# Two fused transformer blocks: gate tiles moved among the stick-breaking items, an own buffer for the first gates, and a new schedule of late rows

## The chip, the cores and the metric

The kernel runs on one core of one Trainium2 chip. TensorE (PE) does the matrix products, VectorE (DVE), ScalarE (ACT) and GpSimd (POOL) the rest, and SyncE (SP) issues most transfers. The metric is the time of one execution in microseconds on the device: 2365.03 us is the median of three runs before the change (2364.62 to 2365.92).

## The reference, cut to what matters

Two blocks work on 512 tokens of width 1024. The first ends in a layer of 16,384 experts: each token scores two lists of 128 keys per head, picks 16 experts for each of 8 heads, and mixes them. The second has two attentions side by side, each followed by a gate.

```python
def peer_ffn(h, wq, sub_keys, u, v):          # 8 heads, top 16 of 128 x 128 experts
    q = (t @ wq).reshape(PEER_BLOCK, PEER_HEADS, 2, PEER_DQ // 2)
    s = jnp.einsum('tpcd,pckd->tpck', q, sub_keys)
    s1, i1 = lax.top_k(s[:, :, 0], PEER_TOPK);  s2, i2 = lax.top_k(s[:, :, 1], PEER_TOPK)
    top, pos = lax.top_k(cand, PEER_TOPK)     # cand = all sums s1 + s2
    g = jax.nn.softmax(top, axis=-1)
    a = jax.nn.gelu(jnp.einsum('tpkd,td->tpk', u[idx], t), approximate=False)
    return jnp.einsum('tpk,tpkd->td', g * a, v[idx])

# second block
o_a = stick_breaking_attention(...)           # w = sigmoid(z) * prod of sigmoid(-z) to the right
y_a = (o_a * jax.nn.silu(sb_z)) @ w_branch_a
o_b = latent_attention(...)                   # softmax; y_b in the same manner
x = x + gate * ((sigmoid(g_a) * y_a + sigmoid(g_b) * y_b) @ w_out)
```

## The kernel before, in words

All products are done in a split form: each float32 operand is cut into a high and a low part, and `split3` (L1081) issues three matmuls, high by high, high by low and low by high. ACT writes the high part (`high`), DVE or POOL the rest (`low`).

**The experts.** 384 of the 512 tokens go through all experts, in groups of two tiles of 128 experts (48 matmuls of 384 columns). `phase_peer` counts groups g from 0 to 75: 4 for an output projection, 8 for the queries, and then 64 for the first half, in which PE multiplies tokens by `u` and ACT takes gelu. The result does not fit into the on-chip memory, so `spill` writes it to DRAM. The second half is `down(g)`, 64 groups again: the gelu is read back, multiplied by the gates (`weigh`, L1713), split and multiplied by `v`. The gates come from DVE's selection (`select`, 16 units up to group 36), from one-hot products (`batch` on DVE, `spread` on PE, 48 batches from group 41 to 68), and from DRAM, where they are kept between (`gate_pair`, L1248, one transfer for two groups).

The last 128 tokens don't take that way. POOL fetches for each of 128 picks the row of `u` or `v` that each token wants (`rows_by_index`, into a ring of five buffers), and DVE takes a dot product with it (`dot`) or adds it up (`row`). Each engine runs one program in order. What decides the place of a pick is `pick_step` (POOL's request), `dot_step` (DVE's dot, a group later) and `row_step` (the rows of `v`), and `batch_place` does so for the gates. Up to group 40 POOL also makes the low part of `u` (L1305), from group 41 on DVE does (L1685).

**The second block.** After the projections the attention goes through 32 pairs of items, one pair in each of `slots` = 34 slots: 16 pairs of stick-breaking items, then 16 of softmax items, with queries against 128, 256, 384 and 512 keys in turn. In slot p PE computes the scores of pair p, then the tiles that `fill[p]` holds, then the values of pair p-2 and the transposes of pair p-1. DVE masks both items, does its part of the fill tiles (`low`, `evac`) and then finishes both items (for stick: a scan L2349 and a product L2352). ACT takes the sigmoids or exponentials (L2188, L2189, L2191), then `high` and its part of the fill. `second_tiles` lists the tiles and their weight pieces in order. A tile `uqm` has 3 products of 128 rows, `kn` and `kv` have 2, `ga` and `sz` 8, `bra` 4; each product is three matmuls of 512 columns. `early` and `late` spread the tiles over the slots by their number.

## Time and profile before

| | us |
|---|---|
| median of three runs | 2365.03 |
| the profiled execution | 2369.11 |
| its span, first to last instruction | 2367.3 |
| PE busy in the span | 2206.1 |
| DVE busy | 1684.8 |
| ACT busy | 918.6 |
| POOL busy | 617.9 |

The first half of the experts ends near 1297 us on the profile's clock, the second near 1827. The attention slots lie between 1967 and 2215. A wait is put down to what came last.

### The profile page before, as it was taken

Reading aid. Unit: us, or ns where it says so; the run is one execution under the profiler, and the core shown is the slowest. Engines: PE = TensorE matmul, PEld = TensorE weight load, DVE = VectorE, ACT = ScalarE, POOL = GpSimd, SP = SyncE. Lnnn points to the kernel's source line nnn. Section 1 sums busy time; section 2 is a strip of 40 time slices with the busy share of each in tenths; the row PEclk is TensorE's granted clock in tenths of the full one; section 3 lists DMA queues with packets and bytes.
Section 4 is the critical chain, followed back from the end, with each engine's and each line's share of the span. In section 5 each row is a group of like instructions: output and inputs, shape, how many; then the busy total and the mean of one; then the engine's idle time right before and its main releaser. Section 6 shows DMA issues by size and latency. Waiting matters only on the chain. (4 is left out here: it accounts for less than half of the span.)

```text
span 2367.3 us, 31784 instructions
## 1 busy us (share of the span) xinstructions
PE 2206.1 (93%) x12629; PEld 1966.4 (83%) x12629; DVE 1684.8 (71%) x2801; ACT 918.6 (39%) x1203; POOL 617.9 (26%) x354
## 2 busy tenths in 40 slices
PE   5999889988999998999999899999999896899997
PEld 2888777866799998999999899999999674576775
DVE  6555677873489999889876778788786656756543
ACT  4222234333233333566653233333333533576323
POOL 0000042322347667233333433333331000000000
PEclk8999999999999999999999999999999898899999
DMA  7567410012237777899999999999995222111222
GB/s 257 206 227 236 154 50 1 1 71 72 89 125 250 242 243 244 300 370 334 364 339 382 361 352 353 351 359 349 350 362 209 82 89 71 54 54 63 80 89 72
DMA packets 178100, 488.69 MB, mean 206 GB/s; under 512 B 13696, under 2 KB 80384, under 8 KB 166432
## 3 DMA queue, kind: packets, MB, share of 16 engines
q1 hardware_dynamic: 141088, 352.43, 43.6%
q0 software_dynamic: 36864, 134.23, 14.7%
q8 instruction: 100, 1.64, 0.3%
q14 instruction: 48, 0.39, 0.1%
HBM read 432.08 MB, written 52.43 MB: 205 GB/s over the span
## 5 line engine op out<-in xcount | busy, mean ns | idle before, releaser
L1087 PE MATMUL ps<-h_high,u_high 128*128 128x384 f32 (+1 forms) x1216 | 429.7, 353 | 21.7 <-POOL u_low L1305 11.9
L1089 PE MATMUL ps<-h_high,u_low 128*128 128x384 f32 (+1 forms) x1216 | 421.3, 346 | 0.0
L1088 PE MATMUL ps<-h_low,u_high 128*128 128x384 f32 (+1 forms) x1216 | 421.2, 346 | 0.0
L1087 PE MATMUL ps<-w_high,v_high 128*128 128x384 f32 x1024 | 343.6, 336 | 10.4 <-DVE w_low L1722 10.4
L1089 PE MATMUL ps<-w_high,v_low 128*128 128x384 f32 x1024 | 342.8, 335 | 0.0
L1088 PE MATMUL ps<-w_low,v_high 128*128 128x384 f32 x1024 | 342.8, 335 | 0.0
L1087 PEld LDWEIGHTS ps<-h_high,u_high 128*128 128x128 f32 x1216 | 231.5, 190 | 35.9 <-POOL u_low L1305 13.8
L1455 ACT ACTIVATE v_high<-v_raw 128x2048 fp32r<-128x2048 f32 x64 | 122.6, 1916 | 346.6 <-PE ps L1089 346.6
L1087 PE MATMUL ps<-h_high,w_high 128*128 128x512 f32 x560 | 226.7, 405 | 22.3 <-DVE w_low L346 7.5
L1089 PEld LDWEIGHTS ps<-h_high,u_low 128*128 128x128 f32 x1216 | 231.1, 190 | 8.1
L1088 PEld LDWEIGHTS ps<-h_low,u_high 128*128 128x128 f32 x1216 | 232.0, 191 | 7.1
L1088 PE MATMUL ps<-h_low,w_high 128*128 128x512 f32 x560 | 220.4, 394 | 0.0
L1089 PE MATMUL ps<-h_high,w_low 128*128 128x512 f32 x560 | 220.3, 393 | 0.0
L1710 DVE TENSOR_TENSOR v_low<-v_raw,v_high 128x2048 fp32r<-128x2048 f32 x64 | 146.7, 2292 | 101.6 <-ACT v_high L1455 101.6
L1293 POOL DMA_INDIRECT mixT<-in_peer_v,row_index x102 | 145.4, 1425 | 252.1 <-DVE row_sum L1754 236.0
L1293 POOL DMA_INDIRECT mixT<-in_peer_u,row_index x103 | 143.2, 1391 | 236.2 <-DVE row_dot L1680 214.3
L1087 PEld LDWEIGHTS ps<-w_high,v_high 128*128 128x128 f32 x1024 | 192.9, 188 | 10.9 <-DVE v_low L1710 9.8
L1088 PEld LDWEIGHTS ps<-w_low,v_high 128*128 128x128 f32 x1024 | 192.9, 188 | 0.0
L1089 PEld LDWEIGHTS ps<-w_high,v_low 128*128 128x128 f32 x1024 | 192.8, 188 | 0.0
L1531 ACT ACTIVATE gelu<-ps 128x384 f32<-128x384 f32 x128 | 62.9, 492 | 322.1 <-PE ps L1089 199.2
L2267 DVE TENSOR_TENSOR w_low<-w_raw,w_high 128x1024 fp32r<-128x1024 f32 x69 | 84.6, 1226 | 133.8 <-ACT w_high L2139 133.6
L1087 PEld LDWEIGHTS ps<-h_high,w_high 128*128 128x128 f32 x560 | 106.4, 190 | 55.1 <-DVE w_low L2267 10.2
(434 smaller groups left out, 4192.5 us busy)
## 6 DMA issues: line engine op xcount, KB each, us to landing
v_raw<-in_peer_v SPq DMA_DIRECT2D x64, 1024.0 KB
w_raw<-in_w SPq DMA_DIRECT2D x99, 512.0 KB, 3.5
u_first<-in_uT SPq DMA_DIRECT2D x32, 1024.0 KB
u_second<-in_uT SPq DMA_DIRECT2D x32, 1024.0 KB
xT<-in_late_w SPq DMA_DIRECT2D x56, 512.0 KB, 4.4
gelu_up<-gelu SPq DMA_DIRECT2D x128, 192.0 KB
gates<-gates_sb SPq DMA_DIRECT2D x12, 2048.0 KB, 12.6
weighted<-gelu_up SPq DMA_DIRECT2D x64, 384.0 KB
```

The source lines that it names most:

```text
L1087: pe.matmul(out, wh, mh, start=start, stop=False)
L1088: pe.matmul(out, wh, ml, start=False, stop=False)
L1089: return pe.matmul(out, wl, mh, start=False, stop=stop)
L1293: pool.indirect_dma_start(out=row_of(total), out_offset=None, in_=table, in_offset=bass.IndirectOffsetOnAxis(ap=row_no[:, n:n + 1], axis=0))\
L1455: act.activation(v_high[:, g % 2], v_raw[:, g % 2], ACT.Copy).then_inc(v_hi, 1)
L1531: act.activation(gel[:, x % 4, :], ps[:, x % 4, 0:DENSE], ACT.Gelu).then_inc(u_ev, 1)
L1710: dve.tensor_tensor(v_low[:, g % 2], v_raw[:, g % 2], v_high[:, g % 2].bitcast(F32), ALU.subtract)\
L2267: dve.tensor_tensor(wlo[:, i % SPLITS, :], raw[:, i % RAWS, :], whi[:, i % SPLITS, :].bitcast(F32), ALU.subtract).then_inc(w_low, 1)
```

## The change: what it does, and the diff

- Picks: 34 picks (40 before) go to the groups 16 to 40, 76 (66) to the groups 41 to 68, and 18 (22) to the end, which now starts at group 68. The last dots fall in group 75, not after it. POOL issues the picks of a group after the low part of the next group, not before it.
- The first batch of gates is one tile later, and the rows of `v` start in the second group of the second half.
- gelu is spilled three groups after it, not four.
- The even gate pairs have a buffer of their own, `first_gates`, so the first can be loaded without waiting for a buffer of `u`. The odd ones use `u_first`.
- ACT and DVE prepare groups 0 and 1 of the second half ahead of the sums over picked rows.
- In the second block the order of the tiles is new: three of the four `sz` and two of the eight `ga` now stand among the stick items; tiles are spread by their products, not their number; `uq` has two heads in a piece, so there are four pieces fewer.
- The score of each item waits for its own bank alone, and DVE masks the item n+2 right behind finishing item n.

```diff
-EARLY, MIDDLE = 40, 66
+EARLY, MIDDLE = 34, 76
-    return GROUPS - 7 + 7 * (n - EARLY - MIDDLE) // (PICKS - EARLY - MIDDLE)
+    return GROUPS - 8 + 7 * (n - EARLY - MIDDLE) // (PICKS - EARLY - MIDDLE)
-    return SPREAD_AT * EXPERT_TILES + m * SPREAD_G * EXPERT_TILES // BATCHES
+    return SPREAD_AT * EXPERT_TILES + 1 + m * (SPREAD_G * EXPERT_TILES - 1) // BATCHES
-    return n * (U_G - 3) // PICKS
+    return 1 + n * (U_G - 4) // PICKS
...
+        first_gates = sb("gates_in", [P, BLOCKS * 2 * GE * TB])
-        gr = [x[:, 0:BLOCKS * 2 * GE * TB].rearrange("p (n j t) -> p n j t", n=BLOCKS, j=2 * GE) for x in u_raw]
+        gr = [x[:, 0:BLOCKS * 2 * GE * TB].rearrange("p (n j t) -> p n j t", n=BLOCKS, j=2 * GE)
+              for x in (first_gates, u_raw[0])]
...
-                if g - 4 >= OUT_G + WQ_G:
-                    spill(g - 4)
+                if g - 3 >= OUT_G + WQ_G:
+                    spill(g - 3)
...
-            spill(GROUPS - 4)
+            gate_pair(0)
             load(0)
-            sp.wait_ge(u_split, OUT_PIECES + WQ_G + U_G - 1)
-            gate_pair(0)
             spill(GROUPS - 3)
             load(1)
             spill(GROUPS - 2)
-            sp.wait_ge(u_split, OUT_PIECES + WQ_G + U_G)
+            sp.wait_ge(u_split, OUT_PIECES + WQ_G + U_G - 1)
             gate_pair(1)
...
-            for x in range(WQ_G + U_G):
+            for x in range(WQ_G + U_G + 1):
...
-                for n in picks_at[x + OUT_G]:
+                for n in picks_at[x + OUT_G - 1]:
...
+            high_v(1)
+            high_w(1)
             act.wait_ge(row_used, PICKS)
             act.activation(row_dot[:], row_dot[:], ACT.Gelu).then_inc(row_gelu, 1)
...
-    for i in range(2):
-        piece("kn", i, [("kn", 4 * i + j) for j in range(4)])
+    piece("kn", 0, [("kn", j) for j in range(4)])
+    piece("ga", 0, [("ga", 0)])
+    piece("sz", 0, [("sz", 0)])
+    piece("kn", 1, [("kn", 4 + j) for j in range(4)])
+    piece("ga", 1, [("ga", 1)])
     piece("kv", 0, [("kv", t) for t in range(4)])
-    for i in range(8):
+    for i in (1, 2):
+        piece("sz", i, [("sz", i)])
+    halfway = len(tiles)
+    for i in (2, 3):
         piece("ga", i, [("ga", i)])
...
+        for first, end, slot, count in ((PROJECTED, HALFWAY, 0, HALF), (HALFWAY, ATTENDED, HALF, slots - HALF)):
+            sizes = [PRODUCTS2[TILES2[j][0]] for j in range(first, end)]
+            for x, j in enumerate(range(first, end)):
+                fill[slot + sum(sizes[:x]) * count // sum(sizes)].append(j)
...
-                if p:
-                    pe.wait_ge(acted, 2 * p)
                 for s in range(2):
+                    if p:
+                        pe.wait_ge(acted, 2 * p - 1 + s)
...
-                dve.wait_ge(scored, 2 * (n // 2) + 2)
+                dve.wait_ge(scored, n + 1)
...
-                if p < PAIRS:
-                    finish(2 * p)
-                    finish(2 * p + 1)
+                for n in (2 * p, 2 * p + 1):
+                    if n < N:
+                        finish(n)
+                    if n + 2 < N:
+                        mask(n + 2)
```

DVE at the end of the experts' first half, before: from the last dot but one to the split of the second group of the second half (`weighted` is the gelu times the gates).

```order
L1680 ISA row_dot 128x1
L1680 ISA mixT,row_dot<-mixT,h_by_token 128x1024
L1680 ISA row_dot 128x1
L1760 TENSOR_TENSOR row_weight<-row_dot,row_gate 128x128
L1757 TENSOR_SCALAR row_sum<-mixT,row_weight 128x1024
L1754 SCALAR_TENSOR_TENSOR row_sum<-h_by_token,row_weight,row_sum 128x1024
L1754 SCALAR_TENSOR_TENSOR row_sum<-mixT,row_weight,row_sum 128x1024
L1718 TENSOR_TENSOR weighted<-weighted,u_first 128x768
L1710 TENSOR_TENSOR v_low<-v_raw,v_high 128x2048
L1722 TENSOR_TENSOR w_low<-weighted,w_high 128x768
```

The same place in the changed kernel:

```order
L1680 ISA row_dot 128x1
L1718 TENSOR_TENSOR weighted<-weighted,gates_in 128x768
L1710 TENSOR_TENSOR v_low<-v_raw,v_high 128x2048
L1722 TENSOR_TENSOR w_low<-weighted,w_high 128x768
L1718 TENSOR_TENSOR weighted<-weighted,gates_in 128x768
L1710 TENSOR_TENSOR v_low<-v_raw,v_high 128x2048
L1722 TENSOR_TENSOR w_low<-weighted,w_high 128x768
L1761 TENSOR_TENSOR row_weight<-row_dot,row_gate 128x128
L1758 TENSOR_SCALAR row_sum<-mixT,row_weight 128x1024
L1755 SCALAR_TENSOR_TENSOR row_sum<-h_by_token,row_weight,row_sum 128x1024
```

The split of the second group moved ahead of the first three rows of `v`, and no dot stands between the splits.

DVE among the stick items, before: one slot with a weight piece, from its masks to the masks of the next.

```order
L2335 TENSOR_TENSOR ps<-ps,causal_mask 128x128 x2
L2267 TENSOR_TENSOR w_low<-w_raw,w_high 128x1024
L2349 SCALAR_TENSOR_TENSOR at_prod<-at_rest,zeros 128x383
L2352 TENSOR_TENSOR at_w<-at_w,at_prod 128x384
L2349 SCALAR_TENSOR_TENSOR at_prod<-at_rest,zeros 128x383
L2352 TENSOR_TENSOR at_w<-at_w,at_prod 128x384
L2335 TENSOR_TENSOR ps<-ps,causal_mask 128x128 x2
```

And in the changed kernel slot 7, with the tile `sz` 0 (`gate_tmp`, `stick_out`, `g_low`):

```order
L2279 TENSOR_TENSOR w_low<-w_raw,w_high 128x1024
L2301 TENSOR_TENSOR gate_tmp<-ps,gate_tmp 128x512
L2303 TENSOR_TENSOR stick_out<-stick_out,gate_tmp 128x512
L2305 TENSOR_TENSOR g_low<-stick_out,g_high 128x512
L2361 SCALAR_TENSOR_TENSOR at_prod<-at_rest,zeros 128x511
L2364 TENSOR_TENSOR at_w<-at_w,at_prod 128x512
L2347 TENSOR_TENSOR ps<-ps,causal_mask 128x128
L2361 SCALAR_TENSOR_TENSOR at_prod<-at_rest,zeros 128x511
L2364 TENSOR_TENSOR at_w<-at_w,at_prod 128x512
L2347 TENSOR_TENSOR ps<-ps,causal_mask 128x128
```

The masks of the next pair stand between and behind the two finishes, and three operations of a gate tile came in.

## Rows read from the trace of the kernel before

**Rows 1.** Waits of PE over the whole execution: who waited for whom, us, times, longest.

```profile
PE ps L1087 <- DVE w_low L2267: 16.4, 13, 5.3
PE ps L1087 <- POOL u_low L1305: 11.9, 9, 2.8
PE ps L1087 <- DVE w_low L1722: 10.4, 2, 9.5
```

**Rows 2.** Busy time by stretch, stick and softmax slots: PE, PEld, DVE, ACT, POOL, PEclk, DMA.

```profile
1967.00:2086.00 119.00, 88.33 (x448) 56.56 (x447) 83.38 (x141) 60.92 (x139) 0.00 (x0) 0.86 0.17 52
2086.00:2218.00 132.00, 127.68 (x708) 97.23 (x707) 77.58 (x195) 81.40 (x145) 0.00 (x0) 1.00 0.20 65
```

**Rows 3.** Timeline of DVE among the stick items: start, us, instruction, idle before and releaser.

```profile
1970.70 0.50 DVE L2335 TENSOR_TENSOR ps<-ps,causal_mask 128x128 f32<-128x128 f32 x2 [5.15 <-PE ps L2072]
...
1999.47 0.50 DVE L2335 TENSOR_TENSOR ps<-ps,causal_mask 128x128 f32<-128x128 f32 x2
2002.84 1.23 DVE L2267 TENSOR_TENSOR w_low<-w_raw,w_high 128x1024 fp32r<-128x1024 f32 x1 [2.87 <-ACT w_high L2139]
...
2006.24 1.22 DVE L2349 TENSOR_TENSOR_SCAN at_prod<-at_rest,zeros 128x511 f32<-128x511 f32 x1
...
2010.28 0.50 DVE L2335 TENSOR_TENSOR ps<-ps,causal_mask 128x128 f32<-128x128 f32 x2
...
2081.02 0.29 DVE L2337 TENSOR_TENSOR ps<-ps,causal_mask 128x128 f32<-128x128 f32 x1
```

**Rows 4.** Waits of DVE from 1966 to 2090 us: us, times, longest.

```profile
DVE w_low L2267 <- ACT w_high L2139: 22.5, 11, 2.9
...
DVE at_prod L2349 <- ACT at_rest L2189: 4.7, 6, 1.0
```

**Rows 5.** Timeline of PE: fill products, the first softmax scores, the last values.

```profile
2041.17 0.39 PE L1088 MATMUL ps<-g_low,w_high 128*128 128x512 f32 x1
2041.40 0.39 PE L1089 MATMUL ps<-g_high,w_low 128*128 128x512 f32 x1
...
2078.64 0.68 PE L2072 MATMUL ps<-mqkv 96*128 96x128 f32 x4 [1.21 <-ACT at_rest L2189]
...
2213.94 1.09 PE L2091 MATMUL ps<-at_wT,mqkv 128*64 128x128 f32 x16
```

**Rows 6.** Timeline of POOL in the selection stage.

```profile
774.18 1.70 POOL L1293 DMA_INDIRECT mixT<-in_peer_u,row_index  x1 [5.20 <-DVE row_dot L1680]
```

**Rows 7.** Timeline around group 40, of DVE, POOL and PE.

```profile
924.37 0.56 DVE L1659 TENSOR_TENSOR peer_sel<-peer_top 128x384 f32<-128x384 f32 x1
...
930.34 4.76 POOL L1305 TENSOR_TENSOR u_low<-u_first,u_high 128x2048 fp32r<-128x2048 f32 x1
...
943.90 1.23 DVE L1680 CUSTOM_DVE_ANT_0 row_sum<-row_sum,h_by_token 128x1024 f32<-128x1024 f32 x1 [3.89 <-DMA row_sum<-in_peer_u,row_index]
...
948.67 1.86 PE L1348 MATMUL ps<-gated_one_hots,one_hots 128*128 128x128 f16 x16 [3.57 <-DVE gated_one_hots L1704]
```

**Rows 8.** Groups of DVE instructions from 700 to 960 us: count, busy us, mean ns, idle before.

```profile
L1644 DVE TENSOR_TENSOR peer_half<-peer_pos,peer_cuts 128x32 uint32<-128x32 uint32 x12 | 20.7, 1728 | 0.4
```

**Rows 9.** Timeline of PE, one of four such waits in groups 41 to 68.

```profile
1011.58 1.08 PE L1348 MATMUL ps<-gated_one_hots,one_hots 128*128 128x128 f16 x16 [0.28 <-issue]
```

**Rows 10.** Timeline of PE, group 72 and the second group of the second half.

```profile
1262.03 0.60 PE L1087 MATMUL ps<-h_high,u_high 128*128 128x384 f32 x1 [2.52 <-DVE u_low L1685]
...
1316.56 0.52 PE L1088 MATMUL ps<-w_low,v_high 128*128 128x384 f32 x1
1316.88 0.52 PE L1089 MATMUL ps<-w_high,v_low 128*128 128x384 f32 x1
```

**Rows 11.** Busy time by stretch, as in rows 2, in the second half of the experts.

```profile
1350.00:1400.00 50.00, 50.00 (x290) 50.00 (x289) 40.42 (x32) 15.90 (x12) 18.49 (x14) 1.00 0.99 356
```

**Rows 12.** Timeline of DVE, a row of `v` ahead of the second group's split.

```profile
1310.74 1.28 DVE L1754 SCALAR_TENSOR_TENSOR row_sum<-mixT,row_weight,row_sum 128x1024 f32<-128x1024 f32 x1 [3.35 <-DMA mixT<-in_peer_v,row_index]
```

**Rows 13.** Timeline of SP: the load of `v` for the third group.

```profile
1304.19 0.38 SPq L1254 DMA_DIRECT2D v_raw<-in_peer_v  x1
```

More of the change, by code:

```diff
@@ L1228, in spill @@
                     sp.dma_start(gelu[g - OUT_G - WQ_G][:, j, :], gel[:, x % 4, :]).then_inc(spilled[x % 4], 16)
-            written = 0
-            for g in range(GROUPS):
-                if g >= 2:
-                    sp.wait_ge(u_split, PIECES_BEFORE + g - 1)
-                if g:
-                    sp.dma_start(u_raw[g % 2][:], raw_of(g)).then_inc(u_in[g % 2], 16)
-                if g == 3:
-                    sp.dma_start(keys[:], k.dram["keysT"]).then_inc(keys_in, 16)
-                if g - 4 >= OUT_G + WQ_G:
-                    spill(g - 4)
-                while written < BLOCKS and g >= batch_place(PER_BLOCK * (written + 1) - 1) // GE + 4:
-                    sp.wait_ge(evac, 2 * PER_BLOCK * (written + 1))
-                    sp.dma_start(k.gates[:, written], gs[:, written % 2]).then_inc(wrote[written % 2], 16)
-                    written += 1
-            assert written == BLOCKS
-            for r in range(2):
-                sp.wait_ge(wrote[r], 16 * (BLOCKS // 2))
             def gate_pair(i):
@@ L1257, in load @@
                 sp.dma_start(w[:, g % 2], gelu[g]).then_inc(w_in[g % 2], 16)
-            spill(GROUPS - 4)
+            written = 0
+            for g in range(GROUPS):
+                if g >= 2:
+                    sp.wait_ge(u_split, PIECES_BEFORE + g - 1)
+                if g:
+                    sp.dma_start(u_raw[g % 2][:], raw_of(g)).then_inc(u_in[g % 2], 16)
+                if g == 3:
+                    sp.dma_start(keys[:], k.dram["keysT"]).then_inc(keys_in, 16)
+                if g - 3 >= OUT_G + WQ_G:
+                    spill(g - 3)
+                while written < BLOCKS and g >= batch_place(PER_BLOCK * (written + 1) - 1) // GE + 4:
+                    sp.wait_ge(evac, 2 * PER_BLOCK * (written + 1))
+                    sp.dma_start(k.gates[:, written], gs[:, written % 2]).then_inc(wrote[written % 2], 16)
+                    written += 1
+            assert written == BLOCKS
+            for r in range(2):
+                sp.wait_ge(wrote[r], 16 * (BLOCKS // 2))
+            gate_pair(0)
             load(0)
-            sp.wait_ge(u_split, OUT_PIECES + WQ_G + U_G - 1)
-            gate_pair(0)
             spill(GROUPS - 3)
@@ L1533, in _ @@
                     high(g + 2 - OUT_G)
+            high_v(1)
+            high_w(1)
             act.wait_ge(row_used, PICKS)
             act.activation(row_dot[:], row_dot[:], ACT.Gelu).then_inc(row_gelu, 1)
-            for g in range(1, U_G):
+            for g in range(2, U_G):
                 high_v(g)
@@ L1742, in _ @@
                         batch(m)
-            weigh(0)
-            low_v(0)
-            low_w(0)
+            for g in range(2):
+                weigh(g)
+                low_v(g)
+                low_w(g)
             for n in dots_at[GROUPS]:
@@ L1964, in width, with first_gate @@
             return (items[n][2] + 1) * P
-        early, late = list(range(PROJECTED, tile_no("ga", 0))), list(range(tile_no("ga", 0), ATTENDED))
         slots = PAIRS + 2
+        soft_ready = tile_no("kv", 3) + 1
         fill = {p: [] for p in range(slots)}
-        for x, j in enumerate(early):
-            fill[x * HALF // len(early)].append(j)
-        for x, j in enumerate(late):
-            fill[HALF + x * (slots - HALF) // len(late)].append(j)
+        for first, end, slot, count in ((PROJECTED, HALFWAY, 0, HALF), (HALFWAY, ATTENDED, HALF, slots - HALF)):
+            sizes = [PRODUCTS2[TILES2[j][0]] for j in range(first, end)]
+            for x, j in enumerate(range(first, end)):
+                fill[slot + sum(sizes[:x]) * count // sum(sizes)].append(j)
+        def first_gate(n):
+            return mo[:, 2 + n, :] if n < EARLY_GA else merged[:, n, :]
         @block.sync
@@ L2036, in tile @@
                         pe.wait_ge(t_low, G0 + 5)
-                    w3, src = weights(j, 0, 3), [(ghi[:, t, :], glo[:, t, :]) for t in range(3)]
+                    w3, src = weights(j, 3 * (n % 2), 3), [(ghi[:, t, :], glo[:, t, :]) for t in range(3)]
                 elif kind == "kn":
@@ L2419, in _ @@
             dve.wait_ge(made, 3)
+            mask(0)
+            mask(1)
             for p in range(slots):
-                if p < PAIRS:
-                    mask(2 * p)
-                    mask(2 * p + 1)
                 for j in fill[p]:
```

29 lines of the change are left out of this document (15 added, 14 removed).

## The prediction

> **What bounds the kernel now.** I read PE's waits first. The longest sums are three: weight splits in the second block (16.4 us), POOL's low parts in the experts' first half (11.9 us), and the split of the first two groups of the second half (10.4 us, one of them 9.5) [rows 1]. Then the busy time by stretch: in the second half of the experts PE is never idle [rows 11], so nothing is to be had there; in the softmax slots it is busy 127.7 us of 132, but in the stick slots 88.3 of 119 [rows 2]. So PE is the bound in the softmax slots and something else is in the stick slots. The timeline of DVE tells what: DVE masks both items, waits 2.87 us for ACT (sigmoids of both items, then the high part of a weight piece), splits it and finishes both items, and the next masks stand right behind [rows 3]. The 16 stick slots are this loop, 1970.7 to 2081.0, 110.3 us.
>
> All sums are against the profiled execution (2369.1 us, its span 2367.3). The median is 4.1 us below that, and I take the same difference off at the end.
>
> **Selection stage, groups 16 to 41.** POOL waits for DVE's dots before it may ask for rows (5.20 us in the row shown [rows 6]) and does PE's low part behind that. The change takes POOL's order apart and leaves DVE fewer dots, so PE's 11.9 us [rows 1] should go. But they come back: at group 38 ACT waits for DVE's last selection, and DVE is full up to there (subtraction of the maxima at 924.37, then the exponential, ACT's high part, and POOL's low part for group 40 from 930.34 to 935.10 [rows 7]). PE arrives sooner and waits there in one piece. What counts is how much sooner DVE ends: dots up to group 36 are 28 in place of 32, 4 x 1.15 us = 4.6 us (each row dot starts 1.15 us after the one before; 1.23 us is the instruction [rows 7]). Behind it stands the wait of 3.57 us for the first gate batch [rows 7]. With the batch one tile later it would be gone, but the pick of group 39 is now asked for only after the low part of group 40. Its dot then stands ahead of the low part of group 41, and such a row took some 8 us from its request (DVE waited 3.89 us of them [rows 7]). By hand, from the time at which group 40 may start: wait for the row 8.3, dot 1.15, low 2.2, dot 1.15, gate parts 0.95, batch 2.45, low 2.2, three dots 3.45, batch 2.45 = 24.3 us to the second batch. PE gets to group 42 some 4 us sooner than before, less 1.5 us for a slow clock after its long wait. I take -3; bounds -9 (the 3.57 and 4.6 both won, and the slow clock not met) to +4 (row and clock both cost once more).
>
> The slow clock is seen in rows: behind the wait of 2.52 us, as behind the one of 9.5 us, about 10 to 12 matmuls start 0.32 us apart, twice the 0.172 us of the steady stretch (290 in 50 us) [rows 10, 11]. Each such wait costs 1.5 to 1.8 us more. Waits up to 1.9 us show none.
>
> **Groups 42 to 68.** 76 dots in place of 66. Before, 10 groups had three dots, now 20 of 28. A group of PE is 48 x 0.172 = 8.3 us and 1.08 per batch [rows 9, 11], so 10.4 with two batches and 9.4 with one. DVE starts its low part 2.5 us after PE starts the group before (ACT's high part lies between); with three dots and a batch it is done at 2.5 + 2.2 + 3.45 + 2.4 = 10.55. Behind a group with two batches PE waits 0.1 to 0.28 us, which is what the four short waits before show [rows 9]; behind a group with one batch, 1.15. The new pattern has four such places (groups 46, 50, 54, 58): 4.6 us, and a little of the short ones. I take +5, bounds 0 and +9 (all 20 groups at 0.45).
>
> **Late rows.** The wait of 2.52 us at group 72 comes from a dot whose row was 13 us under way, behind a burst of four requests and a gate write. Now the burst stands at group 69 and the rows of group 71 are asked for earlier. 2.5 + 1.5 for the clock = -4; bounds -4 and 0.
>
> **Into the second half.** Before: 0.9 and 9.5 us of waits [rows 1] and 1.8 for the clock, 12.2 us. The 9.5 goes, since DVE no longer waits for rows of `v` (3.35 and 3.4 us [rows 12]) ahead of the second split. What is late next is the third group: its `v` is loaded only after all gelu is stored (1304.19 before, some 6 us after the second half began [rows 13]), and PE wants it 16.6 us after the beginning, less the high part 1.9, low part 2.3 and the product's low part 0.95: it has 5 to 6 us to land. 1.4 MB (1 MB of `v`, 0.4 of gelu) at about 200 GB/s beside the row requests is 7 us. I count 0.5 + 0.5 + 2.7 us of waits for groups 0, 1, 2, 1 us of clock and 0.5 later, 5.2 us. Net -7; bounds -12 (nothing is late) and -1. The sooner gates and sooner spill I cost at nothing: the transfers stand in one queue and the DMA engines are busy 0.99 of the time [rows 11], so a sooner issue mostly waits in the queue.
>
> **Stick slots.** The fill of the stick slots grows from 48 to 88 products, at 3 x 0.23 us [rows 5] 27.6 us of PE, into 30.7 us of PE idle time. But DVE is the bound there. Busy on DVE: one more piece (12 for 11, 1.2 us) and three `sz` tiles at 3 x 0.69 us, +7.5 us. Idle on DVE: ahead of a low part it now waits for the sigmoids of one item, not two: about 2.15 for 2.87 us at 512 keys, but there are 11 such waits in place of 9, and one behind two `kn` tiles: +1.2 on the 20 to 22 us [rows 4]. The three `sz` wait for their tile (5.5 us of PE), its sigmoid and the copy between their products: +5.6. The waits for the sigmoids ahead of a finish go: -4.7 [rows 4]. In three slots (12 or 8 products beside little DVE work) PE is last: +4. Together +14, so PE reaches the softmax scores at about 2092, not 2078.6 [rows 5]. Bounds: 0 (the new order of masks hides all) and +27.6 (nothing hidden).
>
> **Softmax slots.** PE took 2078.64 to 2215.0, 136.4 us [rows 5], of which 128 products are 88.3 us. Now 88 products: 60.7, with the same rest of 48.1 is 108.8; four slots have no fill, where the chain of mask, exponential and finish shows, about 0.5 us each: 110.8. -26; bounds -27.6 and, if that chain sets the pace of every slot, 0. Six table loads fewer on ACT (1.28 us each) lie beside PE and give nothing. The attention together: -12.
>
> **Sum.** -3 + 5 - 4 - 7 - 12 = -21: 2348.1 for a profiled execution, 2344 for the median.
>
> **Rivals.**
> 1. *The gates are hidden wholly.* For: 30.7 us of idle PE in the stick slots, and masks that no longer wait for both items. Against: DVE is busy 83 of 119 us there, and its idle time is ACT's chain, which stays. Attention -25 in place of -12: 2331.
> 2. *The experts give nothing.* The waits taken away come back as later ones: DVE at +9 in groups 42 to 68, the third group late by 6 us. For: DMA share 0.99 and DVE busy up to 45 of 50 us. Then -1 from the experts and -12: about 2354 with middle values, up to 2360.
> 3. *DVE is held up by POOL (slower).* The tiny operation L1644, 32 columns, takes 1.73 us on average, more than a scan over 511 columns (1.22) [rows 3, 8]: it waits for something that ends, and 12 of them are 20.7 us. Today POOL is in step with DVE. When POOL's order is taken apart it falls elsewhere. If each of 11 selections lost 2.3 us more, the last would end 25 us later, PE would wait at group 40, and the time would be 2344 + 25 = 2369. It decides from a mean of about 3.5 us for that operation. The Trainium skill (SBUF — State Buffer, section "Who interferes with whom") says that a DVE instruction with two inputs in SBUF and a GpSimd instruction that reads SBUF exclude each other for the whole instruction; by that rule the phase between the two engines sets this price. The long mean agrees with it. It could as well get better.
> 4. *The softmax slots keep their pace (slower).* If mask, table load, exponential and finish take as long per slot as the 8 products did, the 136.4 us stay and the stick slots cost 14: 2344 + 26 = 2370. Against: DVE is busy 77.6 and ACT 81.4 of 132 us there.
>
> **How the numbers follow.** The forecast (2336 to 2354) has 0.52, rival 1 0.15, rival 2 0.16, rivals 3 and 4 together 0.09, and 0.08 goes to sums that end within 0.2% of 2365 (4.7 us, about what a measurement can tell). The range 2328 to 2363 takes in part of rival 1 and nearly all of rival 2. Faster: 0.52 + 0.15 + 0.16 = 0.83; same 0.08; slower 0.09.
>
> **What would show it.** No wait above 1 us on POOL's low parts before group 38, and one of 5 us or more at group 40. Short waits of about 1 us at groups 46, 50, 54 and 58. No wait of 2.5 us near group 72. The second group of the second half starts within 1 us of the end of the first, the third is 1 to 5 us late. First softmax scores 14 us later than the same place before, counted from the first mask, with DVE's low parts still waiting for ACT; then some 111 us to the last values. The forecast is wrong if the stick slots take under 115 or over 135 us, if the softmax slots stay above 120 us, or if L1644 goes above 3 us.

## The result: 0.5% slower, and the profile after

The changed kernel took 2380.91 us (median of 11 runs, 2374.2 to 2385.8), the kernel before 2369.19 us in the same session (2364.4 to 2372.6). The ratio is 1.0047, 95% interval 1.0038 to 1.0057: about 11 us slower. I had forecast 2344 us and gave "slower" 0.09.

Stretches of the two profiled executions, cut at the same work of PE in both:

| from ... to | before | after | difference | forecast |
|---|---|---|---|---|
| start to the fourth score product (L1336, then L1334) | 670.7 | 668.0 | -2.7 | 0 |
| to the transposes of group 40 | 264.9 | 290.5 | +25.6 | -3 (bounds -9 to +4) |
| to the first product of the second half | 362.5 | 367.0 | +4.5 | +1 |
| to the end of the second half | 549.8 | 541.8 | -8.0 | -7 |
| to the first stick scores | 122.2 | 122.0 | -0.2 | 0 |
| stick slots, to the first softmax scores | 108.6 | 128.9 | +20.3 | +14 |
| softmax slots, to the last values | 136.4 | 108.4 | -28.0 | -26 |
| to the end of the span | 152.3 | 152.6 | +0.3 | 0 |

So all of the loss, and more, lies in one stage of the experts, the one in which DVE selects rows. First the waits of PE over the whole execution, which answer to [rows 1]:

```profile
PE ps L1087 <- POOL u_low L1303: 20.0, 6, 8.1
PE ps L1395 <- DVE peer_sel L1739: 17.9, 1, 17.9
...
PE ps L1346 <- issue: 6.9, 7, 2.2
...
PE ps L1087 <- DVE soft_out L2291: 6.9, 3, 3.2
...
PE ps L1087 <- DVE w_low L2279: 2.6, 4, 1.5
...
PE ps L1087 <- DVE w_low L1722: 1.8, 1, 1.8
```

The 9.5 us into the second half are gone (1.8 left), and so are most of the 16.4 us for low parts of weights in the second block. But the waits for POOL's low parts have grown from 11.9 to 20.0 us, and there is a new one of 17.9 us. They stand here (timeline of PE in the changed kernel):

```profile
827.82 0.69 PE L1087 MATMUL ps<-h_high,u_high 128*128 128x384 f32 x1 [8.04 <-POOL u_low L1303]
...
912.97 0.69 PE L1087 MATMUL ps<-h_high,u_high 128*128 128x384 f32 x1 [8.05 <-POOL u_low L1303]
...
958.48 2.18 PE L1395 MATMUL ps<-ident,peer_sel 128*128 128x128 f32 x9 [17.93 <-DVE peer_sel L1739]
```

PE waits for POOL, POOL (8.74 us at 821.38) for DVE's row dots, and DVE waits for nothing in this stage: from 690 us to its end no gap on DVE is above 0.15 us. So the question is why DVE's operations take longer. Groups of DVE instructions from 700 to 960 us, as in [rows 8]; columns are count, busy us, mean ns, idle before. Of the changed kernel:

```profile
L1680 DVE CUSTOM_DVE_ANT_0 mixT<-mixT,h_by_token 128x1024 f32<-128x1024 f32 x26 | 43.0, 1691 | 0.3
L1622 DVE TENSOR_TENSOR peer_indf<-peer_ind,peer_cuts 128x64 f16<-128x64 uint32 x11 | 23.6, 2145 | 0.4
L1644 DVE TENSOR_TENSOR peer_half<-peer_pos,peer_cuts 128x32 uint32<-128x32 uint32 x12 | 17.6, 1463 | 0.4
```

And of the kernel before, beside its L1644 in [rows 8]:

```profile
L1622 DVE TENSOR_TENSOR peer_indf<-peer_ind,peer_cuts 128x64 f16<-128x64 uint32 x11 | 5.3, 478 | 0.4
```

L1622 writes 64 columns and takes 0.23 us when nothing is in its way. Now it takes 2.1 us on average. One case shows what it collides with. DVE, then POOL, in the changed kernel:

```profile
828.52 5.04 DVE L1622 TENSOR_TENSOR peer_indf<-peer_ind,peer_cuts 128x64 f16<-128x64 uint32 x1
833.48 0.68 DVE L1627 TENSOR_TENSOR peer_cand<-peer_val 128x512 f32<-128x512 f32 x1
```
```profile
823.07 4.69 POOL L1303 TENSOR_TENSOR u_low<-u_second,u_high 128x2048 fp32r<-128x2048 f32 x1
827.91 0.96 POOL L1291 DMA_INDIRECT mixT<-in_peer_u,row_index  x1
828.89 4.58 POOL L1303 TENSOR_TENSOR u_low<-u_first,u_high 128x2048 fp32r<-128x2048 f32 x1
```

POOL's low part ends at 833.47, and L1622 ends with it, at 833.56. The same place in the kernel before, DVE and then POOL:

```profile
799.98 0.23 DVE L1622 TENSOR_TENSOR peer_indf<-peer_ind,peer_cuts 128x64 f16<-128x64 uint32 x1
800.12 0.68 DVE L1627 TENSOR_TENSOR peer_cand<-peer_val 128x512 f32<-128x512 f32 x1
...
805.05 1.31 DVE L1644 TENSOR_TENSOR peer_half<-peer_pos,peer_cuts 128x32 uint32<-128x32 uint32 x1
```
```profile
794.56 4.73 POOL L1305 TENSOR_TENSOR u_low<-u_first,u_high 128x2048 fp32r<-128x2048 f32 x1
799.45 0.96 POOL L1293 DMA_INDIRECT mixT<-in_peer_u,row_index  x1 [0.16 <-issue]
800.72 0.94 POOL L1293 DMA_INDIRECT mixT<-in_peer_u,row_index  x1 [0.30 <-issue]
801.67 4.63 POOL L1305 TENSOR_TENSOR u_low<-u_second,u_high 128x2048 fp32r<-128x2048 f32 x1
```

Here L1622 and L1627 fall into the gap between two low parts, and only L1644 meets the end of the second one (806.30). The long runs of MAX8, FIND_INDEX8 and MATCH_REPLACE8 are not longer for lying under a low part: 270 of the 360 in the stage lie wholly under one, and each form stays within 0.03 us.

The ends of the long operations show the same for all of them. In the stage 18 DVE operations before and 20 after are over 0.15 us longer than the shortest of their form. Each ends at a distance behind the end of a low part that depends on its form alone: L1644 0.05 to 0.06 us, L1622 0.08 to 0.09, the row dots 1.08 (they do nearly all their work behind it). And three cases of L1622 like the one shown (at 828.52, 850.87 and 913.68) make up 14.5 us. In each L1622 begins 0.54 to 0.62 us after a row request of POOL, and the low part follows that request at once, 0.97 to 0.99 us after its start. In the kernel before, six L1622 begin 0.51 to 0.53 us after a request, but a second request follows at 1.26 us, and they take 0.22 to 0.23 us. So what stands right behind a request decides over 4.8 us.

This is rival 3 of the prediction, with its price of 25 us for the stage. Only the sign by which I wanted to know it was wrong: I had looked for it in L1644, whose mean fell, from 1.73 to 1.46 us. The stretch came to L1622, to the row dots (1.69 for 1.35 us) and to one L1651 (5.1 us).

**A sum to test with.** I call stretch what the DVE instructions of this stage (from 20 us after the fourth score product to the transposes of group 40) take beyond the shortest instance of their form in all these kernels, 1.22 us for a dot; less than 0.1 us on one operation is not counted. It is 29.3 us before and 60.6 us after; row dots in the stage are 38 and 32. Stage minus stretch minus 1.15 us per dot is 191.9 and 193.1 us. (The texts below that speak of 25.8 and 57.1 leave out one operation, L1739, which takes 4.1 us in most kernels; that it is 0.6 us long was seen only later.) So +31.3 of stretch, -6.9 of dots and +1.2 of rest are the +25.6 us. (Of the 38 dots before, one begins 0.13 us before the end of the stage. Without it the dots give -5.8 and the rest, 193.0 and 193.1, nothing.)

### The profile page after: what moved, and what is told of

It is laid out like the page before. It is cut to its first block and busy times, and to the rows that moved or that the text cites. A ratio compares the mean times of both kernels' runs of the same rounds, so it can differ in the third digit from the quotient of the medians.

```text
span 2379.1 us, 31767 instructions
## 1 busy us (share of the span) xinstructions
PE 2211.7 (93%) x12629; PEld 1972.9 (83%) x12629; DVE 1708.2 (72%) x2797; ACT 910.4 (38%) x1193; POOL 627.2 (26%) x354
## 5 line engine op out<-in xcount | busy, mean ns | idle before, releaser
L2279 DVE TENSOR_TENSOR w_low<-w_raw,w_high 128x1024 fp32r<-128x1024 f32 x65 | 79.6, 1225 | 127.9 <-ACT w_high L2151 127.7
## 6 DMA issues: line engine op xcount, KB each, us to landing
gelu_up<-gelu SPq DMA_DIRECT2D x128, 192.0 KB, 6.4
```

What stands on the lines that cost most here:

```text
L2279: dve.tensor_tensor(wlo[:, i % SPLITS, :], raw[:, i % RAWS, :], whi[:, i % SPLITS, :].bitcast(F32), ALU.subtract).then_inc(w_low, 1)
```

## The experiments

All numbers of stages are from one profiled execution of each kernel (that of both_undone took 2361.1 us, 5.5 above its median); ratios are to the kernel before in the same session, with 95% intervals.

| kernel | time us | ratio | stage to group 40 | stretch | dots | rest |
|---|---|---|---|---|---|---|
| before | 2369.2 to 2370.4 | 1 | 264.9 | 29.3 | 38 | 191.9 |
| changed | 2380.9 | 1.0047 (1.0038-1.0057) | 290.5 | 60.6 | 32 | 193.1 |
| order_undone | 2369.4 | 1.0003 (0.9994-1.0011) | 284.0 | 54.0 | 33 | 192.1 |
| picks_undone | 2366.5 | 0.9992 (0.9983-1.0001) | 270.2 | 34.6 | 37 | 193.1 |
| both_undone | 2355.6 | 0.9946 (0.9931-0.9961) | 264.9 | 29.3 | 38 | 191.9 |
| low_in_four | 2371.5 | 1.0009 (1.0000-1.0018) | 278.4 | 48.4 | 32 | 193.2 |
| low_quarter | 2330.4 (one run) | - | 244.8 | 6.0 | 32 | 202.0, of it DVE waited 5.7 for scores and 4.5 for rows |
| early40_late18 | 2356.0 | 0.9945 (0.9932-0.9959) | 264.9 | 29.3 | 38 | 191.9 |
| one_input | 2356.9 | 0.9950 (0.9937-0.9963) | 265.9 | 32.4 | 38 | 189.8 |
| pairs_even | 2353.5 | 0.9933 (0.9921-0.9946) | 262.4 | 29.1 | 36 | 191.9 |
| pairs_odd | 2340.7 | 0.9879 (0.9863-0.9896) | 252.6 | 20.4 | 35 | 192.0 |
| one_each | 2362.4 (one run) | - | 263.0 | 43.6 | 24 | 191.8 |
| new_order_pairs | 2356.9 | 0.9951 (0.9933-0.9969) | 264.4 | 32.2 | 34 | 193.1 |
| pairs_odd_order_only | 2339.9 | 0.9878 (0.9860-0.9896) | 252.6 | 20.5 | 35 | 191.9 |

(In all kernels with POOL's old order, the kernel before among them, the last of the dots counted begins 0.13 or 0.14 us before the end of the stage. In one_each it waits 4.3 us, which lie behind the stage and are not in its 43.6. Without this dot the rest is 1.15 us more, 193.0 to 193.2 in most of these too.)

**Which part does it?** The three undo POOL's order, the counts, and both:

```
 order_undone:
-            for x in range(WQ_G + U_G + 1):
+            for x in range(WQ_G + U_G):
-                for n in picks_at[x + OUT_G - 1]:
+                for n in picks_at[x + OUT_G]:
 picks_undone:
-EARLY, MIDDLE = 34, 76
+EARLY, MIDDLE = 40, 66
-    return GROUPS - 8 + 7 * (n - EARLY - MIDDLE) // ...
+    return GROUPS - 7 + 7 * (n - EARLY - MIDDLE) // ...
 both_undone: the two together
```

> The changed kernel, with POOL's requests for rows of u put back ahead of the next low part (pick list of group x, not of x-1, and no extra step of the loop). Theory (A): in the selection stage, two-input operations of DVE that meet one of POOL's low parts wait until it ends. That stretch of DVE was 25.8 us in the kernel before and 57.1 us in the changed one, and the length of the stage from the fourth score product to the transposes of group 40 is 195 to 197 us + stretch + 1.15 us per row dot (264.9 us before, 290.5 us after). The order of POOL sets which operations meet. With it undone I expect a stretch of 25 to 40 us, the stage 260 to 274 us, the whole 2353 to 2368 us. Rival (B), the fewer early dots (34 for 40) shift DVE against POOL and are the cause alone: the stretch stays above 50 us, the whole stays at 2378 to 2384 us. Whatever comes, by A the residue of 195 to 197 us holds; by rival (C), the stage is long because rows arrive late, it does not.

> The changed kernel with the counts of picks put back (40 early, 66 middle, 22 late from group 69), POOL's new order kept. Theory A (operations of DVE that meet POOL's low parts wait for their end, the order of POOL decides): stretch stays above 45 us, dots rise by 6 x 1.15 us, the stage 290 to 300 us; groups 42 to 68 get about 5 us shorter and a wait of 2 to 3 us comes back near group 72: the whole 2378 to 2390 us. Rival B (the fewer early dots are the cause): the stretch falls to about 26 us, stage 265 to 270 us, the whole 2350 to 2360 us.

> The changed kernel with POOL's order of requests and the counts of picks both put back; all other parts stay. Both theories A and B: DVE's stretch of about 26 us and the stage of 265 us are back, so the whole is 2381 - 25.6 - (0 to 5 for groups 42 to 68) + (0 to 3 for a wait near group 72) = 2350 to 2358 us, faster than both kernels. Rival C (something else in the changed kernel, such as gelu stored a group sooner, slows the stage): the stage stays above 280 us and the whole above 2370 us.

My theory A as first put, that POOL's order decides, fell: with it undone the stretch is still 54.0 us. The counts bring it to 34.6, both together to 29.3, and the time to 2355.6, under both kernels. The three long L1622 right behind a row request are in order_undone too (14.5 us), and not in picks_undone. Neither theory had the whole time right: order_undone is 9 us under the range of rival B, and picks_undone 6.5 us above it. The rest of 192 to 193 us holds in all three, so rival C is out. The 1.2 us between 191.9 and 193.1 are the dot at the stage's end, as said under the table. What undoing the order gave outside the stage (361.3 for 367.0 us in groups 40 to 75) was not looked into.

**Is it POOL?** Two kernels change the low part itself:

```
 low_in_four:
-                    pool.tensor_tensor(u_low[:, x % 2], u_raw[x % 2][:], ..., ALU.subtract).then_inc(u_split, 1)
+                    for c in range(4):
+                        o, r, h = (t[:, 512 * c:512 * (c + 1)] for t in whole)
+                        last = pool.tensor_tensor(o, r, h, ALU.subtract)
+                    last.then_inc(u_split, 1)
 (whole: the same three operands, their 2048 columns in one dimension)
 low_quarter: the same with range(1), which leaves out three quarters of each low part
```

> The changed kernel with POOL's low part cut to 512 of 2048 columns (three quarters of these low parts are left out, so the output is not the reference's). Theory A (DVE's two-input operations wait for the end of a POOL low part that they meet): a low part is about 1.2 us, no stretch is above 1.5 us and all together under 15 us in place of 60.3; the stage from the fourth score product to group 40 falls from 290.5 us to PE's own 250 to 256 us, and PE's waits on POOL's low parts are under 1 us each. Rival C (the long operations are DVE's own, or rows arrive late): 5-us operations L1622 stay, and the stage stays above 275 us.

> The changed kernel with each of POOL's low parts of 2048 columns (4.6 us) in four operations of 512 columns. Theory A1 (a two-input operation of DVE waits only for the POOL instruction that runs): no stretch above 1.5 us, in sum under 25 us in place of 57.1, the stage 255 to 262 us, the whole 2345 to 2358 us, unless POOL's four take much over 5 us. A2 (POOL keeps its claim over instructions that follow each other at once): stretches of 4 to 5 us stay, stage 285 us or more, the whole 2375 us or more. Rival C (DVE's long operations have nothing to do with POOL): no change of the long operations.

low_quarter settles the cause: one POOL operation was made shorter, and DVE's operations became shorter with it. The stretch falls from 60.6 to 6.0 us, the stage to 244.8. DVE's groups there (the lines stand 4 further down, L1626 is L1622):

```profile
L1631 DVE TENSOR_TENSOR peer_cand<-peer_val 128x512 f32<-128x512 f32 x11 | 7.6, 688 | 0.0
L1626 DVE TENSOR_TENSOR peer_indf<-peer_ind,peer_cuts 128x64 f16<-128x64 uint32 x11 | 4.1, 375 | 0.4
L1648 DVE TENSOR_TENSOR peer_half<-peer_pos,peer_cuts 128x32 uint32<-128x32 uint32 x11 | 2.1, 192 | 0.4
```

The 32-column operation that took 1.73 us before is 0.19 us on average. What is left of the long ones (at most 1.1 us each) ends as before at the same distances behind a low part. low_in_four was to show whether a short POOL instruction is enough with all of the work kept. It lies between my two cases: the stretch is 48.4 us, and in one place DVE got through after one piece, in another not. DVE, then POOL:

```profile
828.73 0.23 DVE L1626 TENSOR_TENSOR peer_indf<-peer_ind,peer_cuts 128x64 f16<-128x64 uint32 x1
828.87 6.19 DVE L1631 TENSOR_TENSOR peer_cand<-peer_val 128x512 f32<-128x512 f32 x1
```
```profile
828.53 0.96 POOL L1291 DMA_INDIRECT mixT<-in_peer_u,row_index  x1 [0.15 <-issue]
829.51 4.99 POOL L1307 TENSOR_TENSOR u_low<-u_first,u_high 128x512 fp32r<-128x512 f32 x4
```

L1631 (0.68 us of its own) began before the first piece and ended at 835.06, behind the fourth (834.50). So a seam between two POOL instructions is not always a place where DVE gets in; when it is, these runs don't tell.

**Only operations with two inputs?**

```
-                dve.tensor_tensor(half[:, 0, :], pos[:], cuts[:, 0:1].to_broadcast(...), ALU.logical_shift_right)
+                dve.tensor_scalar(half[:, 0, :], pos[:], 4, None, ALU.logical_shift_right)
 (L1645 likewise; L1622 and L1646 become dve.tensor_copy; POOL's order and the counts undone, as in both_undone)
```

> The changed kernel with POOL's order and the counts of picks undone, as in both_undone, and four small operations of DVE in each selection turned from two inputs into one: L1622 and L1646 become copies, L1644 and L1645 take their constant as an immediate; the values are the same. Theory A (only DVE operations with two inputs in SBUF wait for POOL): L1644 falls from a mean of 1.3 to 0.2 us, the rest of the wait moves to L1648 (from 1.23 to about 1.7 us), and what is won is the 0.6 us of the three small operations that now run under POOL's low part, some 12 times, and a little at L1622: stage 256 to 260 us in place of 264.9, whole 2347 to 2353 us in place of 2355.6. Rival (any operation of DVE on integers waits for POOL, or L1644 is long by itself): L1644's successor stays at 1.3 us, stage 263 to 266.

This clause of A was wrong. The one-input forms wait as well: L1642 is the old L1644, L1622 the copy.

```profile
L1642 DVE TENSOR_SCALAR peer_half<-peer_pos 128x32 uint32<-128x32 uint32 x12 | 21.8, 1815 | 0.4
...
L1622 DVE CAST peer_indf<-peer_ind 128x64 f16<-128x64 uint32 x11 | 7.0, 634 | 0.4
```

The Trainium skill (SBUF — State Buffer, section "Who interferes with whom") says of copies, casts and scalar operations that they can enter modes which use the port shared with GpSimd, and of reductions on this chip that they never do. I had not weighed that sentence. The traces agree with it. Both forms wait. The reduction of 1.22 us (L1653) meets no low part in the kernel before and in one_input, so these can't tell; but in order_undone one lies wholly under a low part (858.62 us) and takes 1.22 us, and so do six in low_quarter that lie under one with 1.1 us. One thing more shows only here: five of the copies begin 0.52 to 0.54 us into a row request of POOL (0.96 us) and end with it, at 0.43 to 0.44 us, where the two-input form took 0.23 (both_undone). The copy waits for row requests too.

**Number or pattern of early picks?** The selection repeats every two groups. 40 picks over 25 groups have an uneven pattern, 34 another. These kernels set a pattern that repeats every two groups too, or one pick per group:

```
 pairs_odd (EARLY, MIDDLE = 38, 72, POOL's order undone; pairs_even has + 0):
-        return PICK_AT + (SPREAD_AT - PICK_AT) * n // EARLY
+        return PICK_AT + 2 * (n // 3) + (n % 3 + 1) // 2
 new_order_pairs: the same pattern, POOL's new order kept
 one_each (POOL's order undone):
-EARLY, MIDDLE = 34, 76
+EARLY, MIDDLE = 25, 84
```

> POOL's order undone, and 38 early picks set in a fixed pattern: two in each even group, one in each odd one; 72 in the middle, 18 late. Theory A says that the stretch depends on where POOL's low parts stand against the selection, which repeats every two groups: a pattern of two groups gives the same stretch in each selection. With one request between the two low parts of a selection the second ends some 0.9 us sooner and L1644 waits 0.2 to 0.5 us, not 1.1: stretch 18 to 24 us and the stage 253 to 260 us; with two between them it ends later: 30 to 45 us and 266 to 280. I don't know which parity is which; I expect this one to be the good one. Rival B2 (what matters is only how many early dots there are, near 40 or near 34): as with 40, stage 262 to 266.

> The same with two picks in each odd group and one in each even one. Theory A: stretch 30 to 45 us, the stage 266 to 280 us, if the even pattern is the good one, and the other way round; that both parities give the same (within 3 us of the stage) would speak against A's account by phase. Rival B2: stage 262 to 266.

> POOL's order undone, 25 early picks, exactly one in each group 16 to 40, 84 in the middle, 19 late. Fewer early dots still than the 34 of the change, but each selection meets POOL in the same phase. Theory A (the uneven pattern of 34 over 25 groups is what stretches DVE, not the number): no operation L1622 of 5 us at irregular places; either all selections are good or all are bad; with PE as the bound behind it, the stage is 245 to 256 us. Theory B (the fewer early dots, the worse DVE meets POOL): stretch above 55 us, stage 195 + 25 + 55 = 275 us or more. The middle groups have three dots each, so 5 to 12 us are lost there; that is not the question.

> The changed kernel, POOL's new order of requests kept, with the regular pattern of 38 early picks (two in odd groups, one in even ones), 72 middle, 18 late. With the old order this pattern gave a stretch of 17 us and a stage of 252.6. If the pattern is what counts and the order of POOL's queue only moves requests behind the next low part, the stretch is 17 to 25 us, the stage 252 to 262 us, the whole 2341 to 2350 us. If the new order is bad by itself, it shifts the phase: stretch above 30 us, stage above 265 us, whole above 2352 us.

The same 38 picks give a stage of 262.4 or 252.6 us by parity alone: it is the pattern, not the number, though the good parity is the one I had called bad. (pairs_even by itself fits rival B2; pairs_odd does not.) What it does in pairs_odd, DVE and then POOL:

```profile
796.00 0.23 DVE L1622 TENSOR_TENSOR peer_indf<-peer_ind,peer_cuts 128x64 f16<-128x64 uint32 x1
...
801.07 0.28 DVE L1644 TENSOR_TENSOR peer_half<-peer_pos,peer_cuts 128x32 uint32<-128x32 uint32 x1
```
```profile
790.56 4.76 POOL L1303 TENSOR_TENSOR u_low<-u_first,u_high 128x2048 fp32r<-128x2048 f32 x1
795.47 0.96 POOL L1291 DMA_INDIRECT mixT<-in_peer_u,row_index  x1
796.69 4.61 POOL L1303 TENSOR_TENSOR u_low<-u_second,u_high 128x2048 fp32r<-128x2048 f32 x1 [0.26 <-ACT u_high L1447]
```

With one row request between the two low parts of a selection, where the kernel before has two, the second ends at 801.30 and L1644 loses 0.1 us there, not 1.1. one_each is a miss for both theories (the stage takes 263.0 us): its first five selections meet POOL badly (dots of 5.6 us, L1644 up to 4.3 us), and from 800 us on it locks into a phase with 1.1 to 1.2 us lost in each. So a regular pattern doesn't guarantee a good phase, and which one a kernel falls into is not something I can forecast from the counts. New order and good pattern together cost 32.2 us of stretch for 20.4 (new_order_pairs, whole 2356.9 for 2340.7): POOL's new order is bad by itself. It costs 12 us of the stage with this pattern, 5.3 with 40 uneven picks (270.2 for 264.9) and 6.5 with 34 (290.5 for 284.0).

**The late picks.**

```
-EARLY, MIDDLE = 40, 66     (both_undone, 22 late from group 69)
+EARLY, MIDDLE = 40, 70     (18 late from group 68)
```

> The changed kernel with POOL's order undone and 40 early picks as before, but 70 in groups 41 to 68 (66 before, 76 in the change) and so 18 late ones from group 68. The early picks decide how DVE meets POOL (stage 264.8 us as with both parts undone, not 284 to 290), the 18 late ones decide the second half of the experts (541 to 544 us, not 547.6), and 4 dots more in the middle cost 0 to 3 us. Whole: 2355.6 - 4 to 6 + 0 to 3 = 2350 to 2355 us. If the late picks do not matter and the better second half of the changed kernel came from its late first half (transfers had 23 us more to land), the second half stays at 547 and the whole at 2355 to 2358 us.

The second half of the experts takes 539.8 us for 547.6, so the fewer late picks do make it shorter. But groups 40 to 75 take 368.5 for 362.9 us, among it a wait of 5.5 us at 1084.74 where DVE waits 7.9 us for ACT's high part. The sum from group 40 to the end of the experts is 908.3 for 910.5 us, 908.8 in the changed kernel and 912.3 before. The late requests were moved, and their cost with them.

**The second block.** Its two parts alone, on the kernel before, and then the order alone with the rest of both_undone:

```
 attention_order:
+                    if p:
+                        pe.wait_ge(acted, 2 * p - 1 + s)
-                dve.wait_ge(scored, 2 * (n // 2) + 2)
+                dve.wait_ge(scored, n + 1)
 (and finish(n), mask(n + 2) in DVE's loop; the tiles of before)
 attention_tiles: two heads per piece, gates among the stick items, fill by products, and none of these lines
```

> The kernel before with only the second block's new tiles: pieces of two heads, gates among the stick items, fill by products. Masks and scores wait for both items as before. From its first stick scores to its first softmax scores the kernel before takes 108.6 us, the changed one 128.9; to the last values 136.4 and 108.4. If the new order of masks is what hides part of the gates, this kernel takes 132 to 142 us in the stick slots, softmax 108 to 114: whole 2364 to 2378. If the order of masks does nothing, 129 and 108.5: whole 2360 to 2364 us.

> The kernel before with only the second block's new order: scores and masks wait for one item, DVE finishes an item and masks the next one. Tiles as before. If the wait for both items' sigmoids is what the order saves, the stick slots take 100 to 106 us in place of 108.6, the softmax slots 134 to 137: whole 2359 to 2367 us. If DVE's work and the chain through ACT set the pace all the same, 108 to 112 and 136: whole 2368 to 2373 us.

> The changed kernel with POOL's order, the counts of picks and the second block's new tiles undone: what stays are the experts' small parts (first gates sooner in their own buffer, gelu stored a group sooner, splits before row sums, batch a tile later) and the new order of masks and scores in the second block. From first stick scores to last values the order alone took 236.7 us, tiles and order together 237.2 to 240.4, before 245.0. If the tiles bring nothing on top of the order: 2350 to 2355 us, the same as both_undone (2355.6) or up to 4 us less, stick slots 98 to 102. If the tiles matter where the stage before is other: 2357 to 2362.

> All that the runs point to: the experts of the changed kernel with POOL's order undone and the regular pattern of 38 early picks (two in odd groups), 72 middle, 18 late; in the second block the new order of masks and scores with the tiles of before. Stage to group 40 252.6 us, second half of the experts 539 us as in pairs_odd; from first stick scores to last values 235 to 237 us in place of 239. Whole: 2340.7 - 2 to 4 = 2336 to 2340 us. If tiles and order only look alike by chance, 2341 to 2345.

| kernel | time us | ratio | stick slots | softmax slots | both |
|---|---|---|---|---|---|
| before | 2369.2 to 2370.4 | 1 | 108.6 | 136.4 | 245.0 |
| changed | 2380.9 | 1.0047 | 128.9 | 108.4 | 237.3 |
| attention_tiles | 2376.7 | 1.0032 (1.0018-1.0045) | 140.8 | 110.6 | 251.4 |
| attention_order | 2360.2 | 0.9964 (0.9952-0.9976) | 99.5 | 137.2 | 236.6 |
| attention_order_only | 2353.5 | 0.9938 (0.9924-0.9953) | 99.3 | 135.6 | 234.9 |
| pairs_odd_order_only | 2339.9 | 0.9878 (0.9860-0.9896) | 99.4 | 137.2 | 236.6 |

The whole gain of the second block is the order. The tiles alone lose 6.4 us, and on top of the order they bring nothing: 237.3 for 236.6 us. Two pairs of kernels that differ in the tiles alone say so more plainly: both_undone takes 240.4 us there and attention_order_only 234.9 (medians 2355.6 and 2353.5), pairs_odd 238.9 and pairs_odd_order_only 236.6. Of the busy time by stretch (PE, PEld, DVE, ACT, POOL), the stick slots of the changed kernel, then of attention_order:

```profile
1989.25:2118.14 128.89, 108.48 (x532) 76.05 (x533) 82.83 (x141) 60.65 (x133) 0.00 (x0) 0.90 0.15 49
```
```profile
1966.78:2066.26 99.48, 83.03 (x412) 52.87 (x412) 76.85 (x132) 54.51 (x125) 0.00 (x0) 0.86 0.19 59
```

The tiles add 25.5 us of PE work and 29.4 us of time. So nothing of them went into PE's idle time, which is 20.4 us with the tiles (128.9 - 108.5) and 16.5 us without; and the softmax slots give back 28.8 us. Waits of DVE in the stick slots, the changed kernel and then attention_order:

```profile
DVE w_low L2279 <- ACT w_high L2151: 21.6, 12, 2.6
DVE ps L2347 <- PE ps L2084: 21.2, 5, 6.1
```
```profile
DVE w_low L2267 <- ACT w_high L2139: 15.6, 9, 2.1
DVE ps L2335 <- PE ps L2072: 8.6, 4, 5.1
```

So with the tiles DVE waits more for PE's scores, 21.2 for 8.6 us. PE in turn waits for DVE in the same slots (6.9 us of it on `soft_out` L2291, shown above). The two take turns at being the bound; that it goes slot by slot, by whether a slot holds a gate tile or a split, I conclude from the order of the work, and no run tests it.

pairs_odd_order_only joins what was best: 2339.9 us, 1.2% under the kernel before and 1.7% under the changed one (2339.9 / 2380.9). It is hardly better than pairs_odd with the new tiles (2340.7); the sums of 236.6 and 238.9 us had let expect 2 us.

## Why the prediction was wrong

**Selection stage: this step failed**, -3 forecast, +25.6 measured. I gave DVE 4.6 us for its fewer dots and took everything else on DVE as fixed, though the rows showed an operation of 32 columns at 1.73 us on average, and I had named what it waits for. Rival 3 had the mechanism and the place (PE waiting at group 40, 17.9 us in one piece), and I gave it, with another rival, 0.09. That its price of 25 us came out is partly luck: it was 2.3 us in each of 11 selections, which no row gave, and the runs show 31.3 us of stretch in uneven pieces of up to 4.9, less 5.8 for the dots; its whole was 2369, not 2381. Its condition was too narrow: a mean of L1644 above 3.5 us, when any operation that can wait for POOL may be the one. The evidence at hand was enough for more: DVE is the bound of this stage, POOL works 4.6 us of every 8 to 9, and the change alters both engines' patterns. The signs "no wait above 1 us on POOL's low parts before group 38" and "the forecast is wrong if L1644 goes above 3 us" failed, the first by two waits of 8 us, the second by staying silent (1.46 us).

**Groups 42 to 68: right.** Four waits were placed at groups 46, 50, 54 and 58 with 1.15 us each; they are there, every fourth group, 1.27, 1.27, 2.19 and 1.27 us. The first:

```profile
1026.69 1.08 PE L1346 MATMUL ps<-gated_one_hots,one_hots 128*128 128x128 f16 x16 [1.27 <-issue]
```

**Late rows: right.** The wait of 2.52 us near group 72 [rows 10] is gone. Together with the low part of group 41 and the first gate batch (0.52 and 2.79 us of waits) and the slow clock after 17.9 us of waiting (granted 0.50 from 958.4 to 961 us, nine transposes in 2.18 us; 1.00 and 1.20 us before), groups 40 to 75 cost +4.5, where I had +1 and the gate batch in the stage before.

**Into the second half: right in size**, -8.0 for -7. The second group is on time, and the third waits 1.8 us, within my 1 to 5:

```profile
1344.11 0.41 PE L1087 MATMUL ps<-w_high,v_high 128*128 128x384 f32 x1 [1.83 <-DVE w_low L1722]
```

But the cause is partly another. The sooner gates and splits do take away the second group's 9.5 us; yet with 22 late picks the first group waits 5.1 us and the third 4.9 (both_undone). It takes the 18 late ones to get the third down to 1.4 (early40_late18), and those are paid in groups 40 to 75.

**Second block: right in sign, wrong in its reason.** -7.7 for -12. The stick slots cost 20.3 for 14, the softmax slots gave 28.0 for 26. The term that was too small is "in three slots PE is last: +4": DVE's waits for PE's scores rose from 5.8 us to 21.2. And what I ascribed to gates hidden in idle PE is the gain of the order of masks. That the gates are moved at all is worth nothing.

**Rival 4 was wrong**: the softmax slots did not keep their pace (108.4 us, not 136.4). And the middle of rival 2 was mis-added: -1 and -12 give 2352, not 2354.

## What to carry to other kernels

An operation that is several times longer than its columns need is waiting inside itself, and no view of waits lists it. Before changing the pattern of either of two engines that hold each other up, add up that hidden time for all its forms, here 29 us, and treat the whole of it as open in both directions: with POOL's order the same, the pattern of a few dozen requests moved it from 20 to 54 us, and the new order on top brought it to 61. And when a change has two parts in one place, price each alone: here a reordering gave all and the moved work, which looked like the point, gave nothing.

## What the runs showed of the hardware

- DVE operations that start before POOL's low part can still wait for all of it: L1622 began at 828.52, the low part at 828.89, while POOL was issuing a row request (827.91 to 828.87), and L1622 ended at 833.56. In all six such cases (three each in the changed kernel and order_undone) L1622 began 0.54 to 0.62 us into the request and the low part followed 0.97 to 0.99 us after the request's start. Where the low part came 1.1 us or more after it, or another request did, L1622 began 0.50 to 0.56 us into it and took 0.22 to 0.23 us, in every kernel that has this form. In low_in_four three began 0.11 to 0.19 us into a request, with the low part at 0.98, and took 0.22 to 0.23 us too. (The profile's times of POOL are rough, but the same in all cases.) What holds DVE meanwhile is not shown.
- Tensor operations with two inputs, casts and scalar operations waited for POOL's tensor operation; MAX8, FIND_INDEX8, MATCH_REPLACE8 (270 of 360 wholly under a low part in the kernel before, none longer by more than 0.03 us) and TENSOR_REDUCE did not (L1653 under a low part in order_undone and low_quarter: 1220 ns).
- A cast waited for POOL's row request (0.43 us for 0.20, five times in one_input); the two-input form in its place did not (0.23 us in both_undone).
- Cutting a POOL operation of 4.6 us in four (5.0 us together) took the stretch from 60.6 to 48.4 us only.
- Two engines that wait for each other, in semaphores and inside their operations, fall into a phase: with POOL's order the same, the stage lasted 252.6, 262.4 or 284.0 us with 38, 38 and 34 requests in three patterns.
